# Two more pairs of projection blocks by seven products of half blocks: gate blocks 0 to 3 computed in the opening stage instead of in the state-space stage

## What is computed

```python
u = rms_norm(h, norm_mix_pre[layer])
proj = u @ w_in[layer]
sb_qkv, z, xbc_raw, dt_raw, mem_q, gate_logits = jnp.split(proj, SPLIT_POINTS, axis=-1)
...                       # stick-breaking attention, state-space branch (SSD), cross-attention
gates = jax.nn.sigmoid(gate_logits.astype(jnp.float32)).astype(h.dtype)
gates = gates.reshape(b, s, N_BRANCHES, D_MODEL)
merged = (gates[:, :, 0] * (y_sb @ w_sb_out[layer])
          + gates[:, :, 1] * (y_ssd @ w_ssd_out[layer])
          + gates[:, :, 2] * (y_mem @ w_mem_out[layer]))
```

## Time and profile before

| | us |
|---|---|
| median of 3 runs | 2690.98 (2690.51 to 2692.76) |
| the profiled execution | 2689.7 |
| its span, first to last instruction | 2688.0 |
| PE busy | 2598.3 (97%), 12752 matmuls |
| DVE busy | 1856.1 (69%) |
| POOL busy | 1312.0 (49%) |
| ACT busy | 1190.6 (44%) |

### The profile page before, as it was taken

How to read it: one execution, slowest core, us unless ns; L and a number is a source line. 1 busy time by engine, 2 the same in 40 slices (tenths; PEclk the granted TensorE clock), 3 DMA queues, 4 the chain that set the end, 5 groups by cost and what they waited for, 6 DMA issues and landing times. The chain is left out here.

```text
span 2688.0 us, 35509 instructions
## 1 busy us (share of the span) xinstructions
PE 2598.3 (97%) x12752; PEld 2177.9 (81%) x12752; DVE 1856.1 (69%) x2063; ACT 1190.6 (44%) x2098; POOL 1312.0 (49%) x809
## 2 busy tenths in 40 slices
PE   6999999999999999799999899999999999999998
PEld 6888888888888888688888787878887788888886
DVE  6766476777677677498888756654258877768567
ACT  5533144444444444467667544443144222244443
POOL 3333255454454554288887743545600666535224
PEclk9999999999999999899999999999999999999999
DMA  4644443433324341457666653434331444376574
GB/s 159 198 157 167 155 148 96 129 99 114 113 87 134 110 125 56 137 174 211 195 207 202 215 198 134 151 136 149 125 126 55 148 162 158 136 245 210 202 254 147
DMA packets 208108, 411.53 MB, mean 153 GB/s; under 512 B 19648, under 2 KB 100160, under 8 KB 207936
## 3 DMA queue, kind: packets, MB, share of 16 engines
q1 hardware_dynamic: 207936, 409.27, 45.8%
HBM read 289.01 MB, written 120.19 MB: 152 GB/s over the span
## 5 line engine op out<-in xcount | busy, mean ns | idle before, releaser
L1468 POOL TENSOR_TENSOR sb_beta<-sb_beta,sb_rest 128x128 f32<-128x128 f32 (+7 forms) x128 | 163.9, 1280 | 372.3 <-DVE sb_rest L1526 372.3
L1296 PE MATMUL sb_psg<-uh,sb_wl 128*128 128x512 f32 x768 | 309.9, 404 | 0.0
L1296 PE MATMUL sb_psg<-ul,sb_wh 128*128 128x512 f32 x768 | 304.5, 396 | 0.0
L1296 PE MATMUL sb_psg<-uh,sb_wh 128*128 128x512 f32 x768 | 303.0, 395 | 0.0
L3186 PE MATMUL ff_ps<-ff_mh,ff_total 128*128 128x512 f32 x896 | 278.5, 392 | 4.5 <-DVE ff_total L3689 4.5
L1526 DVE TENSOR_TENSOR_SCAN sb_rest<-sb_rest 128x128 f32<-128x128 f32 (+7 forms) x128 | 187.2, 1463 | 115.1 <-ACT sb_rest L1412 114.8
L3186 PEld LDWEIGHTS ff_ps<-ff_mh,ff_total 128*128 128x128 f32 x896 | 169.5, 189 | 40.7 <-issue 5.5
L2331 PE MATMUL first_ps<-uh,mg_wh 128*128 128x512 f32 x480 | 193.7, 403 | 5.8 <-DVE ul L2536 4.9
L2331 PE MATMUL first_ps<-uh,mg_wl 128*128 128x512 f32 x480 | 188.5, 393 | 0.0
L2331 PE MATMUL first_ps<-ul,mg_wh 128*128 128x512 f32 x480 | 188.4, 392 | 0.0
L3186 PE MATMUL ff_ps<-ff_ml,ff_total 128*128 128x512 f32 x448 | 175.4, 391 | 0.0
(11 more groups left out here) (422 smaller groups left out, 7270.3 us busy)
## 6 DMA issues: line engine op xcount, KB each, us to landing
sb_w<-in_w_in SPq DMA_DIRECT2D x48, 512.0 KB, 4.5
scratch_proj<-sb_out SPq DMA_DIRECT2D x48, 512.0 KB, 2.9
ff_w<-in_w_down SPq DMA_DIRECT2D x96, 256.0 KB, 3.6
sb_k<-scratch_qk SPq DMA_DIRECT2D x64, 256.0 KB, 6.0
ssd_arow<-scratch_decay SPq DMA_DIRECT2D x32, 512.0 KB, 5.7
mg_gate<-scratch_proj SPq DMA_DIRECT2D x32, 512.0 KB, 3.5
ff_w<-in_w_up SPq DMA_DIRECT2D x32, 512.0 KB, 3.9
mg_w<-in_w_branch SPq DMA_DIRECT2D x30, 512.0 KB, 4.4
```

What stands on the lines that cost most here:

```text
L1296: last = nc.tensor.matmul(ps_g[:, h], l[:, s, k], r[:, k, h * HALF:(h + 1) * HALF], start=(k == 0 and j == 0), stop=(k == KB - 1 and j == 2))
L1468: nc.gpsimd.tensor_tensor(beta[:, i % 3, 0:cols], beta[:, i % 3, 0:cols], rest[:, i % 3, 0:cols], ALU.mult).then_inc(weighted, 1)
```

## The change

Gate blocks 72 to 75 become two more pairs of the opening stage, behind V's last pair; `PAIRS` goes from 11 to 13. The state-space stage keeps 20 gate blocks, 960 matmuls, and `SLOT` follows as 20 x 48 / 64 = 15. All functions stay as they are; the counts, banks and due slots are derived from these numbers.

```diff
+G_EARLY = 4
...
-    BLOCK_PAIRS = [(b, b + 1) for b in range(2, Z0, 2)]
+    BLOCK_PAIRS = [(b, b + 1) for b in (*range(2, Z0, 2), *range(G0, G0 + G_EARLY, 2))]
...
-        GATES = 3 * KB
+        GATES = 3 * KB - G_EARLY
         PASSES = KB * 3
         SLOT = GATES * 2 * PASSES // (2 * N)
...
-            return w_in[G0 + m] if m < GATES else w_out[m - GATES]
+            return w_in[G0 + G_EARLY + m] if m < GATES else w_out[m - GATES]
...
-                sp.dma_start(proj[G0 + m], out_tile[:, m % 2]).then_inc(g_stored[m % 2], 16)
+                sp.dma_start(proj[G0 + G_EARLY + m], out_tile[:, m % 2]).then_inc(g_stored[m % 2], 16)
```

## The result

The changed kernel takes 2722.33 us (median of 3 runs, 2721.50 to 2724.09) against 2690.98: a ratio of 1.0124, 95% interval 1.0110 to 1.0138, or 31.4 us more. The forecast was 22.3 us more.

What follows compares the result with a forecast made beforehand. A loop of DVE, POOL and ACT, about as long as PE's step, was taken to bound the state-space stage; 38.1 - 0.7 - 6.5 - 8.6 = +22.3 us on 2690.98 gave 2713.3 us, range 2702 to 2725.

Steps and rivals of the forecast that it cites:

- term 1: Opening stage: two more pairs at 19.04 us each, covered by PE, cost +38.1 us.
- term 2: State-space stage: 192 gate matmuls fewer on PE, 43.6 us, of which only -0.7 us would be seen.
- term 4: Start of state-space stage: gate 2's rounding on ACT comes behind the first state's; -8.6 us, bounds 5.7 to 8.9.
- The rival of the clock: State-space stage: PE's gaps lower its clock, its step becomes 12.6 us; +29.5 us, 2720.5; chance 0.10.
- The uncovered pairs: Added pairs don't run covered, or moved gates open another ACT wait on a load; about +38, 2729; chance 0.05.
- the upper bound of 2723: Whole kernel, least favourable sum: 38.1 - 0 - 0 - 5.7 = +32.4 us.
- term 3: State-space stage, POOL: groups 1 to 3 lose one gate low part each, 2.2 us apiece; -6.5 us, bounds 0 to 13.
- my loop: State-space stage: `xd`, `xe`, POOL's work to `aged`, `state`, `sth`, `stl`, next `cb`; 11.37 us without a gate, some 13.5 with.
- The rival that PE ends last: State-space stage: the loop follows PE and gives back up to 43.6 us; net -5.5, 2685.5 us; chance 0.04.
- What I had named as signs: Attention's first matmul at 373.5 us; state-space stage 14 to 18 us shorter; PE busy there some 40 us less.
- The condition under which I called the forecast wrong: Steps with a low part come down towards 11.2 us, or pairs take more than 19.1 us each.

Runs made afterwards that it cites:

- PE's work put back: Changed kernel with one gate product of each slot issued four times, so a slot has 18 products again instead of 15: 1.0115 against the kernel before.
- The order alone: Kernel before with only gate 2's rounding on ACT and its low part on POOL one slot later, behind the first state's rounding: 0.9983.
- The four buffers: Four buffers instead of two for the sums of squares `ssq`: changed kernel 2708.0 us (1.0070 against the kernel before); in the kernel before 0.9970.
- the low parts behind `aged`: POOL's gate low parts moved behind the ageing of the state in the same step: changed kernel 2697.3 us (1.0023); in the kernel before 0.9971.
- both mends: Changed kernel with four buffers for the sums of squares and gate low parts behind the ageing of the state: 2691.0 us, 0.9999 against the kernel before.
- the low parts cut short: Changed kernel with four `ssq` buffers and low parts from the third block on cut to 128 of 1024 columns: one run, 2671.2 us.

## Why the prediction was right, and where it wasn't

**Right.** The sign, the range and the mechanism of the balance: two pairs cost their whole 38.1 us (term 1), and PE's 43.6 us in the other stage are not seen, because a loop of POOL, DVE and ACT sets the pace there (term 2). The run with PE's work put back shows this directly. The start of the stage gained 10.1 us for 8.6 (term 4), 1.2 us over its upper bound; ACT rounds the state first now, and gate 2's load comes behind it. The order alone gave 7.5 of them in the kernel before; with PE's work put back the changed kernel keeps 7.1. So some 3 us are PE's fewer products in steps 0 and 1, of which term 4 had counted 1.4. The rival of the clock was to make PE's steps 12.6 us; the clock did fall to 0.96, but undoing that moves nothing. The uncovered pairs didn't come. That the time stayed under the upper bound of 2723 is partly luck: steps 2 to 31 came out 5.5 us beyond what that bound allowed them, and the start gave 4.4 more than the 5.7 that it had counted.

**The step that failed is term 3**, four low parts fewer: -6.5 us forecast with bounds of 0 and -13, +5.5 measured for steps 2 to 31 together with term 2's -0.7. Two things were wrong in it.

First, the sum took low parts away and left the others where they were. But fewer gate products in a step move all later blocks against the steps: a group has its low parts in other steps. The order showed that, and I read it only for the number of low parts in each group. The third step, 12.9 us without one, got one and takes 16 to 17 us, and the seventh went from 11.4 to 14.4; I had forecast 13.5 for every step that holds one. Besides, the low part that group 3 lost is that of step 31, behind these rows, where only 0.3 us were gained.

Second, my loop lacked a piece. I wrote that POOL does "the squares, the gate's low part if there is one, `skip` and `aged`" behind `xe`, and counted their durations. The squares' 25.6 us of waiting for a store stood in the trace of before, and I didn't ask what a longer wait would be in front of. The four buffers take that out (14 us), the low parts behind `aged` make it harmless (25 us).

How much of the miss is this second piece can be read from the two kernels with four buffers. There groups 1 and 2 are 2.0 and 1.8 us shorter in the changed one (97.61 and 97.55 against 99.64 and 99.35), about the 2.2 of term 3, and steps 2 to 31 are 0.6 us shorter (359.2 against 359.9) instead of 5.5 longer. So 6.2 of the 12.7 us hang on the store's waits. Steps 2 to 7 of group 0 stay 2.4 us longer even then (76.67 against 74.29), and why is open. No run takes products from PE and leaves the low parts in their old steps; what their new places cost is read from the steps alone.

**The rival that PE ends last** was rejected too broadly. Its evidence against, steps of 11.37 us beside PE's 12.53, shows that PE doesn't hold each step; it doesn't show how far a group stands from PE's floor. That distance was 1.2 to 2.9 us (98.15 against 99.40 and 101.03): a chain that has fallen behind PE can run single steps faster than PE and still be held by it over a group. The kernel before was near to being bound by both, and the low parts could only be worth 12 us there. By the rule of the Trainium skill that I weighed there (Perfetto Trace Analysis, section "Identifying the Most-Contended Engine": improve the engine with the highest occupancy first) PE was the one to relieve; for the kernel before as it was, the runs disagree, since steps 2 to 31 became longer with PE relieved and took the same with its work put back. PE is the floor of the kernel before once the low parts stand behind `aged` (98.15 us a group); the changed kernel with both mends still takes 92.7, and comes down to PE's 87.74 only with the low parts cut short.

**What I had named as signs.** Attention starts at 375.63 us instead of 373.5, by the 2.13 us ahead of the pairs. The stage is shorter by 4.6 us (step 0 to 31) instead of 14 to 18. PE's busy time in 411 us fell by 23.4 and not by 40; what is left runs at a lower clock, which I take for the reason, though no run shows how much of it. Steps without a low part in the middle of a group are at 11.36, as said (the second of a group takes 11.35 to 13.92, the last 9.1 to 10.5); those with one are not all at 13.5. The condition under which I called the forecast wrong, steps with a low part near 11.2, did not come; a longer one was not among the signs, and should have been.

Of the 9.0 us between the forecast and the median, 12.7 are terms 2 and 3 in steps 2 to 31, and -1.5 the start; the rest, about -2, is within what single executions differ by (the profiled one alone lies 1.8 above the median).

## What to carry to other kernels

When work is taken out of a stage that runs at an even mean pace, ask where the remaining work moves to in the order, and price each new place, not only the number of operations. A short operation in the middle of a loop between engines can cost about its whole length (2.0 us of 2.4 here) and make the waits in front of it count; the same operation behind the loop's last release cost half as much. Such a move gave 25 us here, where taking four of them out and shifting the others gave less than nothing. Before giving work to a saturated stage in exchange, find the floor of each engine in the other one: make the suspected chain cheap in an experiment and read how far the group falls.

## What the runs showed of the hardware

The stores of the squares, 64 KB each, are issued by SP and land in 6.4 us at the median, 7.7 at the longest; with two buffers in steps of 11 to 13 us, and issued only behind POOL's `skip`, that is on the path, as the run with four buffers shows. A line of the trace's view of that instruction, of the changed kernel:

```profile
DMA to landing us min/median/max: 1.6/6.4/7.7
```

DVE's `xel` takes 0.68 us with the low part out of the way and 2.88 beside POOL's low part of 2.57, in the rows of the two runs above, where it ends 0.55 us behind the low part's own end (1278.81 against 1278.26). The Trainium skill (SBUF — State Buffer, section "SBUF: two separate sides") describes this: a DVE instruction with two SBUF inputs and a GpSimd one that reads SBUF lock each other out for the whole instruction. The rows agree. In the prediction I gave that rule no weight, as the two steps that I compared didn't show it; where the low part stands beside `xel`, the 2.2 us that this adds are as much as a low part was priced at.
